# Second mixer's rotary halves: exchanged by four ScalarE copies a chunk in place of one TensorE product

## What is computed

```python
def rope_tables(n_pos, dim):
    inv = 1.0 / (ROPE_THETA ** (jnp.arange(0, dim, 2, dtype=F32) / dim))
    ang = jnp.arange(n_pos, dtype=F32)[:, None] * inv[None, :]
    ang = jnp.concatenate([ang, ang], -1)
    return jnp.cos(ang), jnp.sin(ang)

def apply_rope(x, cos, sin):
    half = x.shape[-1] // 2
    rot = jnp.concatenate([-x[..., half:], x[..., :half]], -1)
    shape = (1, cos.shape[0]) + (1,) * (x.ndim - 3) + (cos.shape[-1],)
    return (x * cos.reshape(shape) + rot * sin.reshape(shape)).astype(x.dtype)

def dsa_group(q, k, v, qi, ki, wi, cos, sin, cos_i, sin_i, k_top):
    q = apply_rope(q.reshape(bsz, seq, SA_HEADS, SA_DH), cos, sin)
    k = apply_rope(k.reshape(bsz, seq, SA_HEADS, SA_DH), cos, sin)
    qi = apply_rope(qi.reshape(bsz, seq, IDX_HEADS, IDX_DH), cos_i, sin_i)
    ki = apply_rope(ki, cos_i, sin_i)
    ...
        score = jnp.einsum('bqhs,bqh->bqs', rel, wib)
        _, sel = lax.top_k(score, k_top)
    ...
        p = jax.nn.softmax(logits, axis=-1)
```

## Time and profile before

| | us |
|---|---|
| median of 3 runs | 1447.62 (1447.08 to 1450.34) |
| the profiled execution, its own time | 1452.82 |
| its span, first to last instruction | 1451.0 |
| PE busy | 1361.5 (94%) |
| DVE busy | 554.2 (38%) |
| ACT busy | 456.2 (31%) |
| second mixer, layer 1 and layer 2, within the span | 372 to 592 and 930 to 1142 |

### The profile page before, as it was taken

One profiled execution on the slowest core, in us unless ns is written; L12 is line 12 of the kernel. 1 busy time (PEld: TensorE's weight loads), 2 busy tenths in 40 slices (PEclk: granted clock), 3 DMA queues, 4 the chain that ended last, 5 costly groups with the idle time before them and its releaser, 6 DMA issues.

```text
span 1451.0 us, 18735 instructions
## 1 busy us (share of the span) xinstructions
PE 1361.5 (94%) x7343; PEld 859.2 (59%) x7343; DVE 554.2 (38%) x1212; ACT 456.2 (31%) x1007; POOL 38.2 (3%) x58
## 2 busy tenths in 40 slices
PE   6999989999899999989999999799998979999997
PEld 5777567775687877555433343588776654333432
DVE  2234212351477384431212222668485331222114
ACT  3145332453463134321111121564234412112121
POOL 0000000000002000000000000002000000000000
PEclk9999999999999999978999999899999979999999
DMA  9552252331431132554999999132132557999993
GB/s 352 110 166 88 87 206 93 111 116 58 179 117 60 59 124 80 203 204 179 394 422 420 421 422 398 40 113 89 38 138 85 207 203 283 407 421 422 422 422 131
DMA packets 48668, 307.96 MB, mean 212 GB/s; under 512 B 5685, under 2 KB 6197, under 8 KB 16960
## 3 DMA queue, kind: packets, MB, share of 16 engines
q1 hardware_dynamic: 43872, 287.56, 50.3%
q0 software_dynamic: 3520, 9.95, 2.8%
q10 hardware_dynamic: 1184, 9.18, 1.7%
HBM read 300.99 MB, written 8.59 MB: 213 GB/s over the span
## 4 chain that ended last, share of the span: by engine, by line
PE 80%; DVE 13%; ACT 5%; issue 1%; DMA 0%; DVEq 0%; ACTq 0%
PE ps L1010 22%; PE ps L1638 16%; PE ps L1664 8%; PE ps L1256 4%; PE ps L1724 4%; PE ps L1044 4%; PE ps L1703 4%; PE ps L1533 1%; PE ps L1475 1%; DVE projT L2521 1%; PE ps L1218 1%; DVE small L2520 1%; PE ps L1647 1%; PE ps L1481 1%; PE ps L1465 1%
## 5 line engine op out<-in xcount | busy, mean ns | idle before, releaser
L1010 PE MATMUL ps<-hT,ring 128*128 128x272 f32 (+1 forms) x2016 | 482.6, 394 | 7.0 <-ACT projT L1845 3.1
L1010 PEld LDWEIGHTS ps<-hT,ring 128*128 128x128 f32 x2016 | 381.9, 193 | 85.1 <-issue 10.7
L1638 PE MATMUL ps<-ring,arena 128*64 128x512 f32 x384 | 168.8, 604 | 0.0
L1638 PE MATMUL ps<-projT,arena 128*64 128x512 f32 x496 | 167.2, 595 | 1.1 <-DVE arena L2843 1.1
L1664 PE MATMUL ps<-ring,arena 128*64 128x512 f32 x384 | 116.0, 596 | 0.0
L1638 PEld LDWEIGHTS ps<-projT,arena 128*64 128x64 f32 x496 | 49.0, 137 | 101.6 <-issue 101.4
L2842 DVE TENSOR_TENSOR arena<-arena,ps 128x256 f32<-128x256 f32 x32 | 13.5, 421 | 244.5 <-ACT arena L2206 244.5
L1664 PEld LDWEIGHTS ps<-ring,arena 128*64 128x64 f32 x384 | 34.5, 137 | 70.2 <-issue 70.2
L1954 ACT ACTIVATE projT<-ps 128x272 f32<-128x272 f32 x68 | 27.0, 397 | 144.9 <-PE ps L1010 143.4
L1638 PEld LDWEIGHTS ps<-ring,arena 128*64 128x64 f32 x384 | 47.0, 138 | 33.2 <-issue 33.1
L2852 DVE COPY arena<-ps 128x512 f32<-128x512 f32 x64 | 44.1, 690 | 49.9 <-PE ps L1664 49.8
(11 more groups left out here) (476 smaller groups left out, 1674.9 us busy)
## 6 DMA issues: line engine op xcount, KB each, us to landing
ring<-experts SPq DMA_DIRECT2D x96, 1024.0 KB, 11.9
ring<-w_in SPq DMA_DIRECT2D x64, 1024.0 KB, 4.9
projT<-experts SPq DMA_DIRECT2D x62, 1024.0 KB, 12.3
arena<-experts SPq DMA_DIRECT2D x18, 1024.0 KB, 12.9
ring<-w_out SPq DMA_DIRECT2D x16, 1024.0 KB, 4.8
prm<-experts SPq DMA_DIRECT2D x16, 1024.0 KB, 13.4
prm<-params ACTq DMA_DIRECT2D x2, 2048.0 KB, 7.9
prm<-params ACTq DMA_DIRECT2D x2, 1152.0 KB, 10.5
```

Source lines behind the costliest of these rows:

```text
L1010: mm = pe.matmul(ps[:, 5 + j % banks, 0:ncols], w[:, j % 2, k, :], hT[:, k, T - ncols:T], start=(k == 0), stop=(k == KC - 1))
L1638: mm = pe.matmul(ps[64 * e:64 * e + 64, 0, :], xg[:, 4 * h + k, i % 2, 64 * e:64 * e + 64], w[e][:, k // 2, 512 * (k % 2):512 * (k % 2) + ...
```

## The change

The rotation no longer uses PE. In the same place of the list ACT copies the four blocks of 32 partitions crosswise (block q of the target from block q^1 of the chunk) into `rtmp`, which now has two halves used in turn; the sign goes into the table of sines, whose rows for the first half of each head are negative. The constant `rot` goes, and `rope` leaves `SEVEN`, so bank 7 is no longer used by it. Of the four copies only the last signals (`rope_turned`) and only there does ACT wait; from the third rotation on, ACT first waits until DVE is done with the rotation before the last. DVE has its three operations as before, the first now with both operands in SBUF, and it waits for `rope_turned`.

```diff
-SEVEN = ("length", "rope", "tokens", "queries", "values_in", "outputs", "sums")
+SEVEN = ("length", "tokens", "queries", "values_in", "outputs", "sums")
@@ constants
-    put("rot", rot)
-    put("sin", np.tile(np.sin(ang).T, (4, 1)))
+    put("sin", np.tile(np.concatenate([-np.sin(ang).T, np.sin(ang).T]), (2, 1)))
@@ buffers
-        rtmp, _ = more(ONCE_AT + len(ONCE) * SLOT, T)
+        rtmp, _ = more(ONCE_AT + len(ONCE) * SLOT, 2, T)
@@ PE
-                    elif kind == "rope":
-                        i = step[1]
-                        pe.wait_ge(s("projection_copied"), ROPE_CHUNKS[i] + 1)
-                        pe.matmul(ps[:, 7, 0:T], const("rot"), projT[:, ROPE_CHUNKS[i], :], start=True, stop=True)\
-                            .then_inc(s("seven_written"), 1)
@@ ACT
+                    elif kind == "rope":
+                        i = step[1]
+                        if i > 1:
+                            a.wait_ge(s("rope_ready"), i - 1)
+                        for q in range(4):
+                            ins = a.activation(rtmp[32 * q:32 * q + 32, i % 2, :],
+                                               projT[32 * (q ^ 1):32 * (q ^ 1) + 32, ROPE_CHUNKS[i], :], ACT.Copy)
+                        L(ins, s("rope_turned"))
@@ DVE
-                    if kind in ("rope", "queries"):
+                    if kind == "queries":
                         v.wait_ge(s("seven_written"), seven[step])
@@
-                        from_seven(step, v.tensor_tensor(rtmp, ps[:, 7, 0:T], const("sin"), ALU.mult))
+                        v.wait_ge(s("rope_turned"), i + 1)
+                        turned = rtmp[:, i % 2, :]
+                        V(v.tensor_tensor(turned, turned, const("sin"), ALU.mult))
                         V(v.tensor_tensor(x, x, const("cos"), ALU.mult))
-                        V(v.tensor_tensor(x, x, rtmp, ALU.add), s("rope_ready"))
+                        V(v.tensor_tensor(x, x, turned, ALU.add), s("rope_ready"))
```

More of the change, by code:

```diff
@@ L239 @@
                         ("swa_mask", 2 * P), ("mla_mask", 2 * P), ("ident_c", HALF), ("lev_u", HALF), ("lev_l", NLEV * HALF),
-                        ("rot", P), ("rot96", 32), ("cos", T), ("sin", T),
+                        ("rot96", 32), ("cos", T), ("sin", T),
                         ("sel", 4 * P), ("selb", 4 * P), ("caus", T), ("caus2", T), ("desc", 32), ("sel2", 2 * P),
@@ L487, in program @@
                  "state_step_done", "state_ready", "z_sigmoid_ready", "delta_squares",
-                 "delta_rms_ready", "delta_gated", "rope_ready", "index_done",
+                 "delta_rms_ready", "delta_gated", "rope_turned", "rope_ready", "index_done",
                  "index_relu_ready", "index_summed"]
```

## The result

| | before | changed |
|---|---|---|
| median, us | 1448.65 (1447.08 to 1450.34, 4 runs) | 1473.22 (1472.13 to 1474.05, 4 runs) |
| ratio, 95% interval | | 1.0168 (1.0153 to 1.0183) |
| span of the profiled execution, us | 1451.0 | 1472.3 |
| mean granted TensorE clock of the span | 0.965 | 0.951 |

The change costs 24.6 us. The forecast was 1456.6 (+9.0) with a range up to 1465. The sign was right. The time lies 16.6 us above the forecast and 8.2 us above the range; 1.0 of the 16.6 is that the kernel before measured 1448.65 here and 1447.62 before the forecast.

A forecast was written before the change was run, and what follows sets the result against it. PE seemed the bound, but in places the chain ran through DVE and ACT. Path delays of 5.6 us plus 3.4 for slow clock gave +9.0 us: 1456.6 us against the median 1447.6, range 1446 to 1465.

The forecast's parts named there:

- gap 16, convolved values: Layer 1, PE waiting for DVE's convolved values behind the rotation: 2.0 us late, at 470.0 where it was 468.02.
- gap 18, key state: Layer 1, PE's key state waiting for DVE's state update, which stands behind the rotation: 1.4 us late.
- DVE's maximum, gap 24: Layer 1, end of DVE's long stretch from gap 20: 0.3 us late, PE's gains of 2.5 us absorbed.
- gap 26, turning: PE's turning of the probabilities, behind exponentials, eviction, block and DVE's rotation: at 547.4, 1.2 us late against 546.24.
- gap 28, masking: DVE's masking, standing behind a rotation that starts at 565.27: at 566.73 in place of 564.60, 2.1 us late.
- gap 30, turning: PE's turning behind the eviction, block, rotation and norm of gap 29: 576.9 in place of 574.09, 2.8 us late.
- PE gives back at most 24.2 us: PE time saved by removing 26 products and their bank 7 waits: 12.1 us in layer 1, 24.2 for both.
- A block at 1.45 us: Four ACT copies of 0.43 us, overlapping by 0.09: 1.45 us a block, bounds 1.2 and 1.85, 38 us for 26.
- The path from the maximum on: Gaps 25 to 30, chain through ACT and DVE: lateness grows from +0.3 at the maximum to +2.8 us a layer.
- I count one more slow stretch a layer, 1.7 us, two together 3.4.: Clock term: new PE waits in gaps 26 and 30 bring one slow stretch a layer, adding 3.4 us in all.
- more slow stretches: Rival: each of three new waits over 2 us a layer is followed by a slow stretch; 1463.4 us, chance 0.18.
- PE sets the pace: Rival: PE bounds throughout, blocks are ready when DVE and PE ask, all 24.2 us return; 1423 us, chance 0.14.

The follow-up runs named there:

- e2_warm: The changed kernel with idle, unread products on PE ahead of its long waits in gaps 16, 26 and 30: 1460.05 us.
- e1_no_copies: The changed kernel without its 104 ACT copies, DVE multiplying the unexchanged chunk by the sines (rotation wrong): 1432.35 us.
- e9_straight: The changed kernel with its four copies made straight, block q from block q, so nothing is exchanged (rotation wrong): 1474.04 us.
- e3_early: The changed kernel with all ACT copies issued one gap earlier, ahead of the exponentials, DVE's rotation staying in place: 1436.28 us.
- e10_pool: The changed kernel with the four exchanged copies made by GpSimd in place of ACT, once the chunk is evicted: 1435.04 us.

## Why the prediction was wrong

The forecast was a table of lateness by checkpoint, so it can be held against the timelines. Lateness in us of the start of each instruction, counted from PE's first product of the inverse in gap 13 (L1465 before, at 437.86 and 990.43 us; 438.44 and 1001.69 in the changed kernel; 437.60 and 993.48 in `e2_warm`); layer 1 / layer 2.

| checkpoint | forecast | changed | `e2_warm` |
|---|---|---|---|
| gap 16, convolved values | +2.0 | +1.8 / +1.8 | +1.7 / +1.7 |
| gap 18, key state | +1.4 | +2.5 / +2.9 | 0.0 / +0.5 |
| DVE's maximum, gap 24 | +0.3 | +2.0 / +2.1 | +2.4 / -0.5 |
| gap 26, turning | +1.2 | +3.2 / +3.3 | +3.6 / +0.7 |
| gap 28, masking | +2.1 | +7.9 / +9.7 | +4.9 / +3.6 |
| gap 30, turning | +2.8 | +8.9 / +10.6 | +5.8 / +4.6 |
| output product | +2.8 | +10.5 / +12.3 | +5.8 / +4.6 |

- **PE gives back at most 24.2 us.** An upper bound that held; `e1_no_copies` gains 17.5, with 30.7 us of its two stages at 1.2 GHz.
- **A block at 1.45 us: too short.** The forecast took the overlap of 0.09 us from an exponential and the reading of its accumulator. Four copies show none: 1.74 to 1.75 us in the changed kernel and in `e9_straight`, inside my bounds (1.2 to 1.85) and near the far one. Three of the four passes a layer that the prediction counted lie behind the maximum (gaps 25, 28, 29), 3 x 0.29 = 0.9 us a layer. The Trainium skill, "ScalarE: Activation LUTs", section "What ACT_TABLE_LOAD costs", has back-to-back instructions overlap by about 93 ns; no run here shows that for these copies.
- **The path from the maximum on: right.** In `e2_warm` the way from the maximum to the output product grows by 5.8 - 2.4 = 3.4 us in layer 1. Forecast: 2.8 - 0.3 = 2.5, and with the longer block 3.4. In layer 2 it grows by 5.1, and there projection 28 takes 5.62 us (line below), where the kernel before has 3.94: less these 1.7 us, 3.4 again. PE's waits were forecast as near 4, 4.9, 2.4 and 2.7 us and are 3.78, 5.78, 1.70 and 2.92. Ahead of the maximum it fits less well: the key state was forecast at +1.4 and comes at 0.0 and +0.5 in `e2_warm`, and the maximum of layer 1 at +2.4 there, behind a stretch at 1.2 GHz of 10.2 us (488.3 to 498.5) that is 3.4 us long in the kernel before.

```profile
1112.68 5.62 PE L1004 MATMUL ps<-hT,ring 128*128 128x272 f32 x16
```

- **The step that failed: "I count one more slow stretch a layer, 1.7 us, two together 3.4."** Time at 1.2 GHz grew by 44.4 us (17.1 to 61.4), where two stretches like that of the earlier trace rows, 3.4 us each, would be 6.8; filling PE's waits takes 13.2 us off. The table shows where: +1.7 us already at the maximum, then +4.7 and +6.4 us between the turning of gap 26 and the masking of gap 28, where I had +0.9, then 1.7 in each layer behind the wait of 2.92 us in gap 30.
- **Why it was so much.** Too few slow stretches were counted; the price of one was not too low. In the changed kernel the clock is at its lower level in five places of each layer: 6.8 us from the wait of gap 16 on, 3.4 behind the key state's, 10.2 across the two waits of gap 26, 6.8 behind that of gap 27 and 3.4 behind that of gap 30. Against `e2_warm` that is 41 us more at this level, and PE's own work is 13.4 us longer, 1.1 us for each 3.4 us at the lower level; the forecast had 1.7. One could think that the loss feeds itself, since the slow work (the turning at 2.35, the scores at 1.76) is what ACT and DVE wait for next. The waits of PE do not bear that out: they are 39.3 us in the changed kernel and, with the idle products counted as waiting, 40.3 in `e2_warm`, where most of the clock is restored. The slow work lies on the chain and is paid once. Why the clock stays low over both waits of gap 26, no run takes apart.
- **The counter-evidence that I trusted.** I had set layer 2's projection 28, at full speed, against the rival "more slow stretches" and given that 0.18. Its premise was the right one. Its 1463.4 was too low because it had three new stretches a layer of 1.7 us each, where the lower clock lasts some 20 us longer in layer 1 and 24 in layer 2. The Trainium skill, "TensorE: Matmul & The Clock Gate", section "HAM oscillation — how this bites in real kernels", has groups of products behind a wait start cold. The trace of the changed kernel agrees: in or just behind its waits of 3.78, 1.59, 5.78, 1.92 and 2.92 us in layer 1 the granted clock falls to 1.2 GHz.

The sum again, at the output product of both layers: 22.8 us late (10.5 + 12.3). `e2_warm` is 10.4 us late: 5.6 for the path, 1.8 for the longer blocks, and 3.0 that are left (2.1 up to the maximum of layer 1, 1.7 for projection 28 of layer 2, -0.8 up to the maximum of layer 2). The other 12.4 are the clock. By PE's time, the 23.0 us by which the two windows grow are 19.9 of waits more, 10.3 of work less (from the kernel before to `e2_warm`, mostly the 26 products) and 13.4 of work at the lower clock. Another split is possible, since the terms are not independent: by the slope of 23.5 us for each us of a block, the 0.29 us alone, with all it sets off on the clock, would be 6.8 of the 16.6 us missed.

The rival "PE sets the pace" was refuted for this kernel, but its condition was named rightly: a block that is ready when DVE asks for it. With that, in `e3_early` and `e10_pool`, the change wins 14 to 15 us, not 24.

## What to carry to other kernels

When work moves from the engine that is always busy to one with spare time, what counts is the place in that engine's queue and who stands behind it: the same 104 copies cost 41 us right where their result is wanted and 4 us one gap earlier. Price a new wait of PE twice, once as a wait and once for the products behind it at half the clock; and count how long the clock stays low behind all of the waits, old ones that grow too: here it was 44 us more, not 7. A few products that nobody reads, put into a wait that can't be removed, are a cheap test of how much of a loss is clock, and here a gain too, in the kernel before as well.

## What the runs showed of the hardware

- An ACT copy of 272 columns takes 0.428 us on 32 partitions and 0.429 on 128, so cutting by partitions multiplies the time. Four in a row take 1.74 us, no overlap, whether they cross blocks of partitions or not.
- GpSimd copies 32x272 across blocks of partitions in 0.409 us (median; 0.399 to 0.780), about as fast as ACT.
- Loading PE with 14 more products of 128x512 a layer made the kernel 13.2 us faster; the time at 1.2 GHz in the two stages fell from 61.4 to 20.5 us, and PE's waits stayed the same.
- In the kernel before, a wait of PE of 2.16 us is already followed by 3.4 us at 1.2 GHz (468.1 to 471.5 us), and one of 2.00 us in gap 27 of layer 1 too (556.8 to 560.2, 2.1 us after its end), while the same wait in layer 2 (1.99 us) is not.
